# Layer 1's projections, gates and weight splits dealt out anew over its attention iterations; norm scaling moved to VectorE, norm weights applied as rows, the closing norm and the next one made in one chain

## The reference, cut to what matters

```python
def first_block(x, c, w_ada, b_ada, norm_g, ...):
    c_act = jax.nn.silu(c)
    for layer in range(DEPTH):                      # 2 layers
        ada = jnp.einsum('bd,de->be', c_act, w_ada[layer]) + b_ada[layer]
        shift, scale, gate = jnp.split(ada, 3, axis=-1)
        h = rms_norm(x, norm_g[layer]) * (1.0 + scale[:, None, :]) + shift[:, None, :]
        y = even_mixer(h, ...) if layer % 2 == 0 else odd_mixer(h, ...)
        x = x + gate[:, None, :] * y
    return rms_norm(x, final_g)

def odd_mixer(h, w_in, w_out, cos, sin):            # layer 1
    q, k, v, z = jnp.split(jnp.einsum('bsd,de->bse', h, w_in), ...)
    o = moba_attention(q, k, v, cos, sin) * jax.nn.silu(z)   # 16 heads, causal at 256 tokens
    return jnp.einsum('bse,ed->bsd', o, w_out)

def second_block(x, mix_norm_g, w_in, ...):
    u = rms_norm_2(x, mix_norm_g)                   # directly behind rms_norm(x, final_g)
    proj = u @ w_in                                 # q, k, v, convolution and gate columns
    ...
    x = x + merged @ w_o
    hf = rms_norm_2(x, ffn_norm_g) @ w_ffn_in
    x = x + (jax.nn.silu(gt) * up) @ w_ffn_out
```

## Time and profile before

| | us |
|---|---|
| three runs | 822.41, 826.4, 827.5 (median 826.4) |
| the profiled execution | 822.86 |
| its span, first to last instruction | 821.1 |
| PE busy | 763.4 (93%) |
| PEld / DVE / ACT / POOL busy | 651.3 / 495.6 / 384.3 / 47.2 |
| mean granted TensorE clock | 0.973 of 2.4 GHz |

### The profile page before, as it was taken

How to read it: one execution, slowest core, us unless ns; L and a number is a source line. 1 busy time by engine, 2 the same in 40 slices (tenths; PEclk the granted TensorE clock), 3 DMA queues, 4 the chain that set the end, 5 groups by cost and what they waited for, 6 DMA issues and landing times.

```text
span 821.1 us, 12251 instructions
## 1 busy us (share of the span) xinstructions
PE 763.4 (93%) x5042; PEld 651.3 (79%) x5042; DVE 495.6 (60%) x686; ACT 384.3 (47%) x587; POOL 47.2 (6%) x46
## 2 busy tenths in 40 slices
PE   5889799899899999496899999999999999999998
PEld 2577697467687878374799999999887899999886
DVE  1385667654765736646466999964867454554441
ACT  2463465634345436533354435469626553434330
POOL 3100000101200000014200000000003000000000
PEclk9899999999999999699899999999999999999999
DMA  9983446650744622405074545441444355444621
GB/s 367 364 339 151 176 154 254 261 230 29 279 154 172 239 103 103 155 6 199 10 274 179 204 166 197 168 150 52 169 187 164 133 220 205 171 160 184 228 80 51
DMA packets 21542, 145.46 MB, mean 177 GB/s; under 512 B 2464, under 2 KB 2624, under 8 KB 4976
## 3 DMA queue, kind: packets, MB, share of 16 engines
q1 hardware_dynamic: 20736, 142.32, 46.3%
q0 software_dynamic: 480, 1.32, 0.5%
q10 hardware_dynamic: 272, 1.05, 0.3%
HBM read 143.63 MB, written 1.05 MB: 176 GB/s over the span
## 4 chain that ended last, share of the span: by engine, by line
PE 80%; DVE 8%; ACT 4%; issue 4%; POOL 3%; DMA 1%; POOLq 0%; DVEq 0%; ACTq 0%
PE banks L435 22%; PE banks L437 21%; PE banks L436 21%; PE banks L517 4%; DVE WL L1576 3%; PE banks L535 3%; PE banks L598 2%; POOL KT L1085 2%; ACT WH L1106 2%; PE banks L637 1%; POOL RS L1081 1%; PE banks L550 1%; PE banks L605 1%; DMA CST<-in_consts_dram 1%; DVE HL L1613 1%
## 5 line engine op out<-in xcount | busy, mean ns | idle before, releaser
L1576 DVE TENSOR_TENSOR WL<-RAW,WH 128x2048 fp32r<-128x2048 f32 x107 | 243.5, 2288 | 92.8 <-ACT WH L1106 92.2
L1106 ACT ACTIVATE WH<-RAW 128x2048 fp32r<-128x2048 f32 x107 | 203.6, 1906 | 109.4 <-PE banks L437 80.3
L435 PE MATMUL banks<-HH,WH 128*128 128x256 f32 x768 | 218.7, 285 | 3.8 <-DVE WL L1576 3.8
L437 PE MATMUL banks<-HH,WL 128*128 128x256 f32 x768 | 218.0, 284 | 0.0
L436 PE MATMUL banks<-HL,WH 128*128 128x256 f32 x768 | 218.0, 284 | 0.0
L435 PE MATMUL banks<-WH,HH 128*128 128x512 f32 (+1 forms) x336 | 137.5, 409 | 15.8 <-DVE HL L1613 4.8
L435 PEld LDWEIGHTS banks<-HH,WH 128*128 128x128 f32 x768 | 148.1, 193 | 4.5 <-DVE WL L1576 4.4
L436 PEld LDWEIGHTS banks<-HL,WH 128*128 128x128 f32 x768 | 148.1, 193 | 0.1
L437 PEld LDWEIGHTS banks<-HH,WL 128*128 128x128 f32 x768 | 148.1, 193 | 0.0
L437 PE MATMUL banks<-WH,HL 128*128 128x512 f32 (+1 forms) x336 | 133.1, 396 | 0.0
L436 PE MATMUL banks<-WL,HH 128*128 128x512 f32 (+1 forms) x336 | 133.0, 396 | 0.0
(11 more groups left out here) (264 smaller groups left out, 873.9 us busy)
## 6 DMA issues: line engine op xcount, KB each, us to landing
RAW<-in_weights_dram SPq DMA_DIRECT2D x114, 1024.0 KB, 4.9
BIG<-in_weights_dram SPq DMA_DIRECT2D x6, 1024.0 KB, 5.9
ROTS<-in_weights_dram SPq DMA_DIRECT2D x4, 1024.0 KB, 7.1
PROBS<-in_weights_dram SPq DMA_DIRECT2D x2, 1024.0 KB, 9.3
RAW<-in_weights_dram SPq DMA_DIRECT2D x2, 816.0 KB, 7.3
GATE<-in_weights_dram SPq DMA_DIRECT2D x3, 512.0 KB, 7.7
X<-in_x_dram ACTq DMA_DIRECT2D x1, 1024.0 KB, 6.1
QT<-in_weights_dram SPq DMA_DIRECT2D x1, 1024.0 KB, 14.0
```

What stands on the lines that cost most here:

```text
L435: pe.matmul(out_, lhsT=w[0], rhs=x[0], start=start, stop=False, **more)
L437: return pe.matmul(out_, lhsT=w[1], rhs=x[0], start=False, stop=stop, **more)
L1106: do(act.activation(WH[:, s % SPLIT_RING, 0:kb * width], RAW[:, slot[n] % RAW_RING, 0:kb * width], ACT.Copy), high_done)
L1576: do(dve.tensor_tensor(WL[:, s % SPLIT_RING, w], RAW[:, slot[n] % RAW_RING, w], WH[:, s % SPLIT_RING, w], ALU.subtract), low_done)
```

## The change

- **Layer 1 dealt out anew.** PE's extras become: two token projections in iteration 0, one in 1, one in 2, a feature projection in 3, a row of conditioning and `v1_1` of t = 0 in 4, `v1_1` of t = 1 in 5, a feature projection in 6, one and the other row of conditioning in 7, the gate rows and `wo1_0` in 8, `wo1_1` in 9. ScalarE's and VectorE's extras, the order of the pieces, and the iteration in which the heads' output is written (`high_step`: 7 at the earliest) follow. The first four heads are made ahead of the other work of an iteration.
- **Layer 0.** The compressed keys' GELU (`hidden`, `hidden_tanh`) moves from ahead of the attention into iteration 0, behind the split of `za.0`; `lows(16)` goes from iteration 6 to 7; the heads' output is written from iteration 6 + o instead of four at once in 6; the 16 products of the compressed scores alternate between the two halves of partitions and two banks.
- **Norm scaling on VectorE.** n1, n2 and n3 are scaled on VectorE right behind the power. For n2 and n3 the norm's weights are a row over all partitions (MIXR, FFNR, by two new transfers on GpSimd's queue), multiplied in with the scaling, so that PSUM is read straight into HH (ScalarE, two copies) and HL (VectorE, two subtractions). For n2 PE waits half by half.
- **nf and n2 in one chain.** VectorE makes X·final_g into XH; ScalarE squares X and XH; `stat_twice` makes both means, one power of two columns follows, and one instruction the scaled rows for n2. `closing_norm`, which rewrites X, comes behind all of n2.
- **Output of the second block's branches.** `low_merged` runs one step later, with the split of piece `branch_first + 8` ahead of the last.

```diff
@@ piece_table
-    t += rows("q1_0", "k1_0", "v1_0") + z1[:1] + ada(1, 4) + rows("q1_1", "k1_1") + last[:1] + ada(1, 5)
-    t += last[1:] + z1[1:] + list(out_[0]) + list(out_[1])
+    t += rows("q1_0", "k1_0", "v1_0") + z1[:1] + rows("q1_1", "k1_1") + z1[1:2] + ada(1, 4) + last + z1[2:]
+    t += ada(1, 5) + list(out_[0]) + list(out_[1])
@@ high_step
-            return max(last_pair(layer, o) + 3, 6)
+            return max(last_pair(layer, o) + 3, 7) if layer else max(last_pair(layer, o) + 3, 6 + o)
@@ tensor
-                for half in range(2):
-                    bank = ps.open(pe, "proj", f"cmp.{half}")
-                    r = slice(HD * half, HD * half + HD)
-                    for t in range(NT):
-                        for j in range(B_HEADS // 2):
+                banks = [ps.open(pe, "proj", f"cmp.{half}") for half in range(2)]
+                for t in range(NT):
+                    for j in range(B_HEADS // 2):
+                        a = (t * (B_HEADS // 2) + j) * NC
+                        for half, bank in enumerate(banks):
...
-            attention(1, {0: [lambda: by_tokens("q1_1", 0), lambda: conditioning_row(1, 4, "out"),
-                              lambda: by_tokens("q1_1", 1)],
-                          1: [lambda: head_turn("q1_1", 0), lambda: by_tokens("k1_1", 0),
-                              lambda: head_turn("q1_1", 1), lambda: by_tokens("k1_1", 1)],
-                          2: [lambda: head_turn("k1_1", 0), lambda: by_tokens("v1_1", 0),
-                              lambda: conditioning_row(1, 5, "out"),
-                              lambda: head_turn("k1_1", 1), lambda: by_tokens("v1_1", 1)],
-                          3: [lambda: by_features("z1_0", 1)], 4: [lambda: by_features("z1_1", 0)],
-                          5: [lambda: by_features("z1_1", 1)], 6: [lambda: gate_rows(1)],
-                          8: [lambda: half_tokens("wo1_0", 0, 0, use="y1.0.0", heads=KB)],
+            attention(1, {0: [lambda: by_tokens("q1_1", 0), lambda: by_tokens("q1_1", 1)],
+                          1: [lambda: head_turn("q1_1", 0), lambda: by_tokens("k1_1", 0),
+                              lambda: head_turn("q1_1", 1)],
+                          2: [lambda: by_tokens("k1_1", 1), lambda: head_turn("k1_1", 0)],
+                          3: [lambda: by_features("z1_0", 1), lambda: head_turn("k1_1", 1)],
+                          4: [lambda: conditioning_row(1, 4), lambda: by_tokens("v1_1", 0)],
+                          5: [lambda: by_tokens("v1_1", 1)], 6: [lambda: by_features("z1_1", 0)],
+                          7: [lambda: by_features("z1_1", 1), lambda: conditioning_row(1, 5)],
+                          8: [lambda: gate_rows(1), lambda: half_tokens("wo1_0", 0, 0, use="y1.0.0", heads=KB)],
@@ gpsimd
-                if name[:2] in ("n1", "n2", "n3"):
-                    pool.wait_ge(rstds, n + 1)
-                    t = int(name[-1])
-                    pool.tensor_scalar(XH[:, t, :], X[:, t, :], RS[:, n, 0:1], None, ALU.mult).then_inc(x_hat, 1)
@@ scalar
+            def high_norm(n, t):
+                for half in range(2):
+                    bank = ps.wait_filled(act, f"n{n}.{t}.{half}")
+                    do(act.activation(HH[:, 4 * half:4 * half + 4, t * P:(t + 1) * P],
+                                      bank[:, :].rearrange("p (b s) -> p b s", b=4), ACT.Copy), ht_high)
@@ vector
+            attention(1, {0: [lambda: gate(0), lambda: lows(odd_first + 10), lambda: rotate("q1_1", 0), lambda: lows(odd_first + 11)],
+                          1: [lambda: rotate("q1_1", 1), lambda: lows(odd_first + 12), lambda: rotate("k1_1", 0),
+                              lambda: lows(odd_first + 13)],
...
             add_output(1, 0, 1)
-            stat("nf", 0)
-            closing_norm(0)
+            gained(0)
+            dve.wait_ge(mixr_in, 16)
+            do(dve.tensor_tensor(MIXR, MIXR, FING[:, :], ALU.mult))
+            do.after()
+            stat_twice(0)
+            gained_hat("n2", 0, MIXR)
             lows(mix_first + 1)
-            stat("n2", 0)
             add_output(1, 1, 0)
-            evict_norm(2, 0)
-            low_tile(2, 0)
+            low_banks(2, 0)
             add_output(1, 1, 1)
+            gained(1)
             lows(mix_first + 2)
-            stat("nf", 1)
-            lows(mix_first + 3)
-            closing_norm(1)
+            stat_twice(1)
+            gained_hat("n2", 1, MIXR)
             lows(mix_first + 4)
-            stat("n2", 1)
-            evict_norm(2, 1)
-            low_tile(2, 1)
+            low_banks(2, 1)
+            for t in range(NT):
+                closing_norm(t)
```

185 lines of the change are left out of this document (113 added, 72 removed).

## The result

| | before | changed |
|---|---|---|
| median | 826.72 us (4 runs) | 802.64 us (4 runs, 799.13 to 804.05) |
| ratio | | 0.9707, 95% interval 0.9666 to 0.9749 |
| profiled execution | 822.86 us | 801.96 us |

What follows compares the result with a forecast made beforehand. PE's own work was taken as the floor, with only its waits and slow-clock stretches winnable. Terms sum to 23.6 us, giving 799.3 beside the profiled execution and 802.8 beside the median; forecast 801.0 us, range 794 to 812.

Steps and rivals of the forecast that it cites:

- Layer 0, iteration 0: PE's 3.83 us wait for the split of za.0 falls to 0.5 and the slow clock behind it goes: −4.0 us.
- Compressed scores: Layer 0's 32 score matmuls with alternating halves: −0.3 us, bounds 0 and −1.8, since PE then waits behind VectorE's peaks.
- Iteration 7: Layer 0: moving `lows(16)` removes a 2.93 us wait and slow clock, −4.5; later transfers cost 2.1; together −2.4 us.
- Norm n1: Faster power and scaling shorten the chain by 4.0 us; PE's 2.19 us wait for a bank nearly goes; together −2.9 us.
- Layer 1: Attention: 14.2 us of idle and slow clock, less 2.3 for iteration 2's new wait and 1.9 at the end: −10.0.
- my own rule of 1.6 us for each such wait: Behind each PE wait of this size (3.83, 2.36 us), some 1.6 us of slow work is counted.
- Norms nf and n2: Behind layer 1: chain 5.0 us shorter, less 2.57 for two closing norms ahead of `qk_norm(0)`: about −2.5 us.
- Norm n3: Waits of 1.21 and 1.18 us and half a microsecond of scaling go, −2.9; scaled row ahead of split, +1.4: −1.5.
- The first: Rival, chance 0.22: layer 1's iterations 2, 3 and 5 each wait for a split, norms give nothing: 808, up to 813.
- The second: Rival, chance 0.11: the norms' clock stays high and compressed scores free 1.8 us instead of 0.3: 794 to 797 us.
- Slower: Rival, chance 0.03: late splits delay SyncE's transfers, 4.2 us per iteration; slower than the median from four such iterations on.
- The fourth: Rival, chance 0.02: layer 1's waits were only carried by the weights' arrival; only the norms change, 822 to 830 us.

## Why the prediction was right, and where it was off

The number is close (802.64 for 801.0), and part of that is luck. By the two traces the terms add up to 20.9 us won where 23.6 were forecast: layer 1 fell short by 3.4, iteration 7 by 1.2, n1 by 0.9 and the scores by 0.4, and the norms behind layer 1, n3 and the start gave 3.2 more than their terms. The forecast was put between the sum beside the profiled execution (799.3) and the sum beside the median (802.8), and the fall of the clock in layer 1, worth 2.4 to 2.7 us, came in this profile and not in others of the same instructions.

**Layer 0, iteration 0: right.** Wait 0.51, clock at 1.00 behind it, 0.8 us lost at the copy of QT; -4.0 forecast and -4.0 measured, and the undoing gives the same number.

**Compressed scores: the sum right, the step wrong.** "VectorE was idle for only 0.34 us ahead of its next peaks" was to be the cover. The runs show the second bank's drain by ScalarE in its place.

**Iteration 7: right in kind, short by half in size.** The term "I charge most of it, 2.1" measured 3.0: the later transfers are waited for twice, in iterations 8 and 9 (1.30 and 1.29), not once, because four of them land one behind the other at a DMA share of 0.93.

**Norm n1: the failed step is "so this wait nearly goes (−2.0)".** It is 2.20 as it was 2.19. PE comes to the transposes earlier, and transposes, eviction, rests and rotation follow in the same order as before, so the whole group moved forward unchanged. That the wait moves with the group is read from the order, no run shortens the group. What was won are the two waits for GpSimd's rows ahead of it, 1.14 and 1.73, against a new one of 1.02 for the rests of the first half. The 1.9 us of the power, though confirmed as contention, were covered.

**Layer 1: the mechanism right, its largest term mis-sized, one term left out.** By the prediction's own sign ("If layer 1's stage is not 8 us shorter, the prediction is wrong in its largest term") it was wrong here: the stage is 6.6 us shorter, and its clock 0.96, not near 1. The new wait in iteration 2 was priced at 2.3 and is 2.13; the end was left 1.9 and has 1.56. But "14.2 − 2.3 − 1.9" charges the new wait without the slow clock behind it, against my own rule of 1.6 us for each such wait. In the changed kernel's two profiles the fall cost 2.4 and 2.7 us more: 6.6 us were won, not 10.0. Where it did not fall, 9.0 were. The rule itself reads more into the rows than they hold: behind the wait of 2.19 at 224.36 the kernel before ran at 1.00.

**Norms nf and n2: the direction right, the size off by two errors that partly cancel (-2.5 forecast, -4.2 measured).** The forecast took the chain of the second half only; the first half's wait of 2.84 us ahead of its transposes also went, -3.0 to that point. Against it stand 2.35 us for a split behind `gained(1)`, which I did not see, and 4.75 ahead of q2 where I said 2 to 4. The mechanism for that one was right: the rewriting of X held up the drain by 2.6 us, as its removal shows. That the shorter chain is what let the waits of 2.84 and 4.39 go is read from the two traces; no run undoes it alone.

**Norm n3: mis-sized.** The new waits there are 0.43 and 0.37, not 1.4; 2.4 us were won and not 1.5.

**The rivals.** The first (waits come back in several iterations) happened in one iteration, not in three. The second (more is won) did not: the norms' clock did not stay high (0.89), and the scores gave nothing. Slower did not happen: behind the start of the kernel the only waits for transfers are the two of layer 0. The fourth, that the waits in layer 1 were carried by the weights' arrival, is refuted by the undoing of the distribution, which brings them back. The range held because the terms missed on both sides. The chance of 0.93 for faster should have been 0.95, the sum of the three cases that it names, and 8 × 0.46 is 3.7, not 3.6; neither changes the forecast.

## What to carry to other kernels

A wait is worth its length only if nothing else on the same chain ends just behind it: ask for each removed wait what the next wait is measured from (n1's 2.2 us moved with the group, n2's stretch was equally long at either clock). Work of an engine off the critical path belongs into that engine's own waits: the rewriting of X cost 2.6 us ahead of one instruction, 2.5 us and a clock fall ahead of another, and nothing between two splits. And when a kernel's executions differ by 1%, compare stretches of the trace cut at the same instruction, with the clock beside them, and not spans.

## What the runs showed of the hardware

- The same wait of 2.12 to 2.14 us of PE was followed by the clock at 1.2 GHz in four profiles and not in six. In one set of four executions the scatter from 798.7 to 808.1 us goes with the mean clock (0.989 to 0.976); in the other set it does not order them.
- The clock also fell to 1.2 GHz at 178.20 us, behind 7.7 us in which PE was busy throughout.
- GpSimd's power of one column took 0.56 us alone and 2.54 us beside VectorE's split with two operands in SBUF, in three kernels alike, and ended 0.43 us behind the split.
- Four pieces of weights issued within 1.6 us landed at 155.2, 157.9, 160.4 and 164.1 us, with the DMA engines at 0.93.
- Alternating the two halves of partitions brought 32 matmuls of 15 columns from 3.59 us down to 1.96.
